# Third block of a two-network kernel on one Trainium2 core: five projection slabs as seven block products, probabilities scaled on ScalarE, another order at the feed-forward start and at the end

## The reference

```python
h = rms_norm_2(x, mix_norm_g[l]) * (1 + scale_m) + shift_m
proj = h @ w_in[l] + b_in[l]                       # 1024 -> 2816 columns
q_a, k_a, v_a, q_h, f_h, i_h, g_h = jnp.split(proj, IN_OFFSETS, axis=-1)
attn = sliding_window_gqa_with_sinks(q_a, k_a, v_a, sinks)   # p = e / (e.sum + exp(sink - m))
rec = hgrn2_chunkwise(q_h, f_h, i_h, lower_bounds)
rec = rms_norm_2(rec, hgrn_out_g) * jax.nn.silu(g_h)
x = x + gate_m * (concatenate([rms_norm_2(attn, attn_out_g), rec]) @ w_out[l])
h = rms_norm_2(x, ffn_norm_g[l]) * (1 + scale_f) + shift_f
u, v = jnp.split(h @ w_up[l], 2, axis=-1)          # 2 x 2816 columns
u = causal_depthwise_conv(u, conv_w[l], conv_b[l])
x = x + gate_f * ((jax.nn.silu(u) * v) @ w_down[l])
return rms_norm_2(x, final_norm_g)
```

## Time and profile before

| | |
|---|---|
| median of 3 runs (lowest to highest) | 1099.87 us (1098.5 to 1101.79) |
| profiled execution, its own time | 1098.37 us |
| its span | 1096.5 us |
| TensorE busy in the span | 1073.6 us, 98% |
| VectorE busy | 788.8 us, 72% |
| ScalarE busy | 332.0 us, 30% |

### The profile page before, as it was taken

The page is one execution under the profiler, slowest core; times in us unless marked ns, Lnnn a source line. Parts: engine busy times, 40 slices in busy tenths (PEclk is TensorE's granted clock), DMA queues, the critical chain, the costliest instruction groups (busy, mean ns, idle before and its releaser), DMA issues.

```text
span 1096.5 us, 18062 instructions
## 1 busy us (share of the span) xinstructions
PE 1073.6 (98%) x7396; PEld 972.1 (89%) x7396; DVE 788.8 (72%) x1359; ACT 332.0 (30%) x783; POOL 24.5 (2%) x83
## 2 busy tenths in 40 slices
PE   7999999999999999999999999999999999999997
PEld 4788888999999977888899999998889889999997
DVE  2477768888898848544779889887474288887755
ACT  3243324111111245663511111117343342222101
POOL 1000240000000000000000000000000000000000
PEclk9999999999999999999999999999999999999999
DMA  9899936898878662381868878774432165953411
GB/s 347 275 385 343 316 106 249 297 319 282 319 276 300 191 77 77 98 258 57 299 214 323 309 280 304 263 251 151 154 116 77 46 204 171 290 184 106 151 62 39
DMA packets 163011, 234.79 MB, mean 214 GB/s; under 512 B 8770, under 2 KB 137842, under 8 KB 162930
## 3 DMA queue, kind: packets, MB, share of 16 engines
q1 hardware_dynamic: 162572, 233.54, 63.2%
q10 hardware_dynamic: 357, 0.12, 0.0%
HBM read 232.19 MB, written 1.44 MB: 213 GB/s over the span
## 4 chain that ended last, share of the span: by engine, by line
PE 88%; DVE 8%; ACT 2%; issue 1%; ACTq 0%; DMA 0%; DVEq 0%
PE PS L850 34%; PE PS L780 13%; PE PS L896 13%; PE PS L808 7%; PE PS L971 6%; PE PS L1096 3%; PE PS L772 1%; PE PS L1358 1%; DVE hT L1978 1%; PE PS L793 1%; PE PS L701 1%; PE PS L1441 1%; DVE scratch L2400 1%; PE PS L1300 1%; PE PS L1049 1%
## 5 line engine op out<-in xcount | busy, mean ns | idle before, releaser
L780 PE MATMUL PS<-hT,slots 128*128 128x256 f32 x752 | 165.3, 380 | 0.8 <-ACT hT L1535 0.8
L780 PEld LDWEIGHTS PS<-hT,slots 128*128 128x128 f32 x752 | 142.1, 190 | 21.7 <-issue 2.9
L896 PE MATMUL PS<-act,slots 128*128 128x256 f32 x704 | 159.8, 380 | 0.4 <-DVE act L2123 0.4
L1902 DVE SCALAR_TENSOR_TENSOR ada_acc<-ada_slots,cond,ada_acc 128x1024 f32<-128x1024 f32 x119 | 152.4, 1280 | 4.8 <-DMA ada_slots<-in_ada_w 0.5
L896 PEld LDWEIGHTS PS<-act,slots 128*128 128x128 f32 x704 | 130.5, 190 | 18.9 <-issue 1.6
L1573 ACT ACTIVATE PS<-PS 128x128 f32<-128x128 f32 x180 | 53.5, 297 | 299.7 <-PE PS L850 299.7
L850 PE MATMUL PS<-oT,slots 128*128 128x128 f32 x960 | 126.9, 275 | 2.0 <-ACT PS L1573 2.0
L850 PE MATMUL PS<-hT,slots 128*128 128x128 f32 x960 | 127.0, 275 | 0.0
L850 PEld LDWEIGHTS PS<-hT,slots 128*128 128x128 f32 x960 | 119.6, 192 | 2.4
L850 PEld LDWEIGHTS PS<-oT,slots 128*128 128x128 f32 x960 | 116.8, 192 | 2.3 <-issue 2.3
L850 PE MATMUL PS<-oT,scratch 128*128 128x128 f32 x960 | 117.1, 275 | 0.0
(11 more groups left out here) (347 smaller groups left out, 1337.0 us busy)
## 6 DMA issues: line engine op xcount, KB each, us to landing
ada_slots<-in_ada_w SPq DMA_DIRECT2D x144, 512.0 KB, 8.6
slots<-in_ffn_w_up SPq DMA_DIRECT2D x44, 1024.0 KB, 11.9
slots<-in_ffn_w_down SPq DMA_DIRECT2D x22, 1024.0 KB, 5.0
slots<-in_w_up SPq DMA_DIRECT2D x22, 1024.0 KB, 5.2
slots<-in_sb_w_in SPq DMA_DIRECT2D x11, 1024.0 KB, 13.2
slots<-in_w_in SPq DMA_DIRECT2D x11, 1024.0 KB, 5.3
slots<-in_dsa_w_in SPq DMA_DIRECT2D x10, 1024.0 KB, 5.4
ada_slots<-in_w_down SPq DMA_DIRECT2D x2, 2816.0 KB, 12.4
```

The costliest lines, as they stand in the source:

```text
L780: last = mm(PS[:, bank, half * T:half * T + T], slot[s][:, k, m * P:(m + 1) * P], x[:, k, :], start=k == 0, stop=k == KC - 1)
L896: last = mm(PS[:, c // 2, (c % 2) * T:(c % 2) * T + T], w[:, j_odd * D + c * P:j_odd * D + (c + 1) * P], act[:, j_odd, :], start=start and ...
L1902: ins = dve.scalar_tensor_tensor(dst, ada_slot[k][:, :], c, dst, ALU.mult, ALU.add)
```

## The change

Five slabs of the third mixer no longer run as 16 matmuls of 256 columns but as 28 matmuls of 128 columns (`seven`), after the same scheme of block sums as the feed-forward. VectorE makes the sums of the activations once (`block_x_sums`) and of each slab's weights (`block_w_sums`), and puts the seven products together (`block_collect`). The probabilities are scaled by ScalarE (`window_scale`), the gate's SiLU reads VectorE's collected rows (`block_gate`). In the third feed-forward VectorE starts the sums of the first weight set before the last output slab, makes `norm` and `input_sums` before the two raw chunks, TensorE no longer waits for unit 3, and ScalarE takes the first two SiLUs after the first seeds. The output slabs 1 to 4 lie in slots 3, 4, 2, 5 where they lay in 2, 3, 4, 5. At the end one transpose moves into the last chain, `token_rows(0, 0)` moves ahead of the last `take`, and ScalarE's queue issues one of the four output transfers.

```diff
-OUT_SLOTS = ((3, 4, 5, 2), (3, 4, 5, 2), (2, 3, 4, 5))
+OUT_SLOTS = ((3, 4, 5, 2), (3, 4, 5, 2), (3, 4, 2, 5))
...
+                arrived(s)
+                fill(u)
+                product(0, w[:, 0:HALF, 0:P], b11, frees=frees)
+                product(1, w[:, HALF:KC, 0:P], b21)
+                pe.wait_ge(block_x_ready, 1)
+                pe.wait_ge(block_w_ready, bk("block_w_ready").next())
+                product(2, block_w[buf][1], block_x[1])
+                product(3, block_w[buf][0], block_x[0]).then_inc(block_half, 1)
+                product(4, w[:, 0:HALF, P:2 * P], block_x[2])
+                product(5, block_w[buf][2], b22)
+                product(6, w[:, HALF:KC, P:2 * P], block_x[3]).then_inc(unit_full[u], 1)
...
-            pair(3, 0, None)
-            tokens(4, 1, 3)
+            seven(3, 0, 0)
+            seven(4, 1, 1, frees=3, by_token=True)
             window_turn(4)
-            tokens(5, 0, None)
+            seven(5, 0, 2, by_token=True)
             window_mix(0, 1, 5)
             window_scores(1, None)
-            pair(0, 0, None)
-            pair(1, 1, 0)
+            seven(0, 0, 0)
+            seven(1, 1, 1, frees=0)
...
-                    if n == 0 and not j_odd:
+                    if l < 2 and n == 0 and not j_odd:
                         was_read(3)
...
+                    if p == 0:
+                        for raw_odd in (0, 1) if l == 2 else (1,):
+                            chunk(raw_odd)
+                            skip(2 + raw_odd)
...
+            def window_scale():
+                for m in range(2):
+                    act_e.wait_ge(inverse_ready, bk("inverse_ready").next())
+                    for e in range(2):
+                        for tt, (lo, hi_) in enumerate(((0, P), (P, 384))):
+                            x = esp[:, 2 * m + e, lo:hi_]
+                            last = act_e.activation(x, x, ACT.Copy, scale=psum_p[:, m, tt, e:e + 1])
+                    last.then_inc(p_ready, 1)
...
-            gate(hg, GH0, 0, ACT.Silu, 0)
-            gate(hg, GH0, 1, ACT.Silu, 1)
+            window_scale()
             window_probs()
+            block_gate(hg, GH0, 0, 0, 0)
+            block_gate(hg, GH0, 1, 1, 1)
...
+                act_e.wait_ge(block_taken, i + 1)
...
+            act_e.wait_ge(o_scaled, 1)
+            act_e.dma_start(out[0, P:2 * P, 0:512], oT_flat[:, 1024:1536]).then_inc(out_stored, 16)
...
+                if l == 2:
+                    weight_sums(2, 0, (1,))
+                    norm(1)
+                    input_sums()
+                    for odd in range(2):
+                        normalise(odd)
+                        chunk(odd, odd, raw[:, odd, 0, :], raw[:, odd, 1, :])
+                    weight_sums(2, 1, (0,))
+                    for odd in range(2):
+                        product(odd, normalised=True, j=odd)
+                    last_chunks()
+                    return
...
+                link(dve.tensor_tensor(s1, a21, a22, ALU.add))
+                dve.tensor_tensor(a21, a11, a21, ALU.subtract)
+                link(dve.tensor_tensor(s2, s1, a11, ALU.subtract))
+                dve.tensor_tensor(s4, a12, s2, ALU.subtract).then_inc(block_w_ready, 1)
...
+                dve.wait_ge(block_half, bk("block_half").next())
+                link(dve.tensor_copy(rows[:, 5 * P:6 * P], flat[:, 0:P]))
+                link(dve.tensor_tensor(rows[:, 0:8 * P].rearrange("p (a b) -> p a b", a=2)[:, :, 0:P], two(flat[:, P:3 * P]),
+                                       spread(rows[:, 5 * P:6 * P]), ALU.add))
                 full(u)
+                link(dve.tensor_tensor(two(rows[:, 6 * P:8 * P]), two(flat[:, 3 * P:5 * P]), spread(u2), ALU.add))
+                dve.tensor_tensor(rows[:, P:3 * P], flat[:, 5 * P:7 * P], rows[:, 6 * P:8 * P], ALU.add)
+                dve.tensor_tensor(rows[:, 3 * P:4 * P], flat[:, 3 * P:4 * P], rows[:, 7 * P:8 * P], ALU.add).then_inc(unit_read[u], 1)
...
-            values(0, 1)
+            values(0, 1, 1)
             decayed_halves(4)
-            values(1, 0)
+            block_w_sums(GH0, 0)
+            values(1, 0, 2)
             window_out(0, 1)
             window_max(1)
-            skip(0)
-            skip(1)
+            block_w_sums(GH0 + SLAB, 1)
             decayed_halves(5)
             decayed_near(6)
             window_norm()
+            for i in range(2):
+                block_collect(i, i)
+                dve.nop().then_inc(block_taken, 1)
...
-            out_projection(2, units=OUT_UNITS[2])
+            out_projection(2, units=OUT_UNITS[2], before_last=lambda: weight_sums(2, 0, (0,)))
```

More of the change, by code:

```diff
@@ L346, in build @@
         down_w_landed = {}
+        block_landed = {}
         def rows(ap):
@@ L968, in chain @@
                     for i in range(PAIRS):
-                        if i == PAIRS - 1 and late is not None:
+                        if i == late_at and late is not None:
                             late()
@@ L1006, in down_blocks @@
                     pe.wait_ge(s_sums_ready, 4 * b + 4)
[L1007 to L1010, removed]
+                    chain(b, 6, s_sum[2], acts[:, :, 1, P:T], late=turn_corner if b == 3 else None, late_at=8)
                 pe.wait_ge(x_turned, 12)
@@ L1350, in pair, with seven, product @@
                 project(2 * u + 1, s, 1, hT).then_inc(unit_full[u], 1)
-            def tokens(s, u, frees):
+            def seven(s, u, buf, frees=None, by_token=False):
+                w, flat = slot[s], PS[:, 2 * u:2 * u + 2, :].rearrange("p b n -> p (b n)")
+                b11, b21, b22 = hT[:, 0:HALF, 0:P], hT[:, HALF:KC, 0:P], hT[:, HALF:KC, P:T]
+                def product(r, a, b, frees=None):
+                    for k in range(HALF):
+                        lhs, rhs = (b[:, k, :], a[:, k, :]) if by_token else (a[:, k, :], b[:, k, :])
+                        last = mm(flat[:, r * P:(r + 1) * P], lhs, rhs, start=k == 0, stop=k == HALF - 1, skip_group_check=True)
+                        if k == 0 and frees is not None:
+                            last.then_inc(slot_used[frees], 1)
+                    return last
                 arrived(s)
                 fill(u)
[L1356 to L1362, removed]
+                product(0, w[:, 0:HALF, 0:P], b11, frees=frees)
[7 more added lines that the diff above has]
+                product(6, w[:, HALF:KC, P:2 * P], block_x[3]).then_inc(unit_full[u], 1)
             def window_keys(frees):
@@ L2003, in ffn, with token_rows @@
+            def token_rows(tt, half):
+                lo = half * 512
+                dve.scalar_tensor_tensor(oT_flat[:, tt * D + lo:tt * D + lo + 512], PS[:, 4 + 2 * tt + half, :], rtok[:, tt:tt + 1],
+                                         final_g[:, lo:lo + 512], ALU.mult, ALU.mult).then_inc(o_ready, 1)
             def ffn(l):
                 both = l < 2
[L2006 to L2022, removed]
@@ L2054, in normalise @@
                     full(2 + odd)
-                    if not odd:
+                    if not odd and both:
                         dve.wait_ge(rstd_ready, bk("rstd_ready").next())
@@ new lines, in block_w_sums @@
+            def block_w_sums(slab, buf):
+                s, landed = block_landed[slab]
+                dve.wait_ge(slot_loaded[s], landed)
+                w, (s1, s2, s4) = slot[s], block_w[buf]
+                a11, a12, a21, a22 = (w[:, k * HALF:(k + 1) * HALF, m * P:(m + 1) * P] for m in range(2) for k in range(2))
+                link(dve.tensor_tensor(s1, a21, a22, ALU.add))
+                dve.tensor_tensor(a21, a11, a21, ALU.subtract)
+                link(dve.tensor_tensor(s2, s1, a11, ALU.subtract))
+                dve.tensor_tensor(s4, a12, s2, ALU.subtract).then_inc(block_w_ready, 1)
@@ L2562, in window_out, with values @@
+            def values(i, u, buf):
+                rows = block_collect(u, buf)
+                bias = vi_bias[:, P + i * SLAB:P + (i + 1) * SLAB].rearrange("p (m c) -> p m c", m=2)
+                dve.tensor_tensor(hi_t[:, :, i * SLAB:(i + 1) * SLAB].rearrange("p t (m c) -> p m t c", m=2),
+                                  rows[:, 0:4 * P].rearrange("p (m t c) -> p m t c", m=2, t=2),
+                                  bias.unsqueeze(2).to_broadcast([P, 2, 2, P]), ALU.add)
             def window_out(i, u):
```

139 lines of the change are left out of this document (98 added, 41 removed).

## The result

The changed kernel took 1093.02 us (median of 4 runs, 1092.73 to 1093.89), the kernel before 1099.69 beside it (4 runs, 1098.5 to 1101.79): a ratio of 0.9939, 95% interval 0.9921 to 0.9956. The profiled execution took 1092.73 where that of before took 1098.37: 5.6 less, in a span of 1091.0 for 1096.5. One execution in the whole document, of its last kernel, was slow (1589.76 us at a mean granted clock of 0.657), and no comparison uses it.

What follows compares the result with a forecast made beforehand. The prediction took TensorE, busy 98% of the span, as the bound. Gains of 1.05 (mixer), 0.8 (feed-forward's start) and 0.8 (end) sum to 2.7 us: 1097.2 us against the median of 1099.87, 8-in-10 range 1094.3 to 1100.3.

Steps and rivals of the forecast that it cites:

- what bounds the kernel now: Whole kernel: TensorE, busy 98% of the span; idle entries read only at the third feed-forward's first product and the end.
- the sum of 2.7 us: Total predicted gain: 1.05 in the third mixer, 0.8 at the third feed-forward's start, 0.8 at the kernel's end.
- The slabs: Third mixer: 28 narrow matmuls take 6.25 us for 6.91, saving 0.66 a slab, 3.3 for five if TensorE never waits.
- VectorE's side: Third mixer: block sums cost 2.66 us and a collection 1.96, making unit 0 free at 815.8.
- the wait of 0.4: Third mixer, before the first gate slab: TensorE waits 0.4 us for VectorE to free unit 0, to 815.9.
- ScalarE's side: Third mixer: scaling, table load, gates and `cross` make TensorE wait 1.3 us before level 2; the mixer gains 1.05 of 3.3.
- Rival 3: Level 2 and the feed-forward's second slice: a table switch costs twice its load, another 1.28 us each; gain 0.1, chance 0.05.
- The feed-forward's start: Third feed-forward: the 1.43 us wait goes, new waits of 0.45 and 0.15 arise; gain 0.8, bounds 0 to 1.43.
- The end: End of the kernel: ScalarE's second root follows its own last sum, at about 1091.3 instead of 1092.13; gain 0.8 us.
- The two queues: End of the kernel: the last two 256 KB transfers leave from two queues at once, worth up to 0.3 us or nothing.
- the first: Rival: small instructions cheaper, collections at 1.5, VectorE never late; mixer gains 2.1, total 4.6, 1095.3 us; chance 0.33.
- The second: Rival: VectorE bounds the mixer at 3.65 us a collection; kernel 2.4 slower, 1102.3 us; chance 0.07.

Runs made afterwards that it cites:

- its last kernel: The changed kernel with levels copied ahead of the gates and the weight sums behind the sum of squares: 1090.46 us, ratio 0.9923 to the kernel before.

## Why the prediction was wrong

**The step that failed** is the first one, what bounds the kernel now. It said that TensorE has idle entries at two places, and costed ScalarE's new order only in the third feed-forward; in the first two it stood at nothing, without a reason. But the page of the kernel before has 2.0 us idle behind ScalarE's L1573 in one of its groups of seven-block products (L850), and those lie in the first two feed-forwards. The section on the reference says that the first two blocks are not touched, and that is wrong: the edit `if l < 2 and p:` changes both of their feed-forwards. Taking it back costs 2.3 to 2.7 us, alone on the kernel before it gives 2.7. Without it the sum of 2.7 us was nearly right (the traces give 3.0 for the same three terms); with the 2.56 it would have been 5.3.

**The slabs**: 6.25 each, as priced. **VectorE's side**: the collection takes 1.89 with the step to the next (810.77 to 812.66) for my 1.96, the sums 2.66 as priced. All small prices together were 0.6 us too high by unit 0's release (812.66 + 2.56 = 815.2 on the time axis of the kernel before, for 815.8), so the wait of 0.4 there did not arise (no idle entry at 812.95); the second turn lost 0.3, not 0.5. From the changed kernel's VectorE timeline:

```profile
810.77 0.28 DVE L2671 COPY oT<-PS 128x128 f32<-128x128 f32 x1
811.09 0.42 DVE L2672 TENSOR_TENSOR oT<-PS,oT 128x256 f32<-128x256 f32 x1
811.54 0.42 DVE L2675 TENSOR_TENSOR oT<-PS,oT 128x256 f32<-128x256 f32 x1
812.00 0.42 DVE L2676 TENSOR_TENSOR oT<-PS,oT 128x256 f32<-128x256 f32 x1
812.35 0.28 DVE L2677 TENSOR_TENSOR oT<-PS,oT 128x128 f32<-128x128 f32 x1
812.66 0.69 DVE L2684 TENSOR_TENSOR ada_acc<-oT,vi_bias 128x512 f32<-128x512 f32 x1
```

**ScalarE's side**: right in place and nearly in size. The wait before level 2 is 1.51 for 1.3. On the same axis level 2 starts at 834.6 for 834.8, so ScalarE was 0.2 early, and TensorE was ready at 833.1 for 833.5, so 0.4 early. ScalarE's timeline:

```profile
828.12 1.28 ACT L1841 ACT_TABLE_LOAD   x1
829.41 0.91 ACT L1841 ACTIVATE ada_acc<-scratch,pcol 128x256 f32<-128x256 f32 x2
830.35 0.91 ACT L1841 ACTIVATE ada_acc<-ffn_work,pcol 128x256 f32<-128x256 f32 x2
831.29 0.60 ACT L1882 ACTIVATE fm<-PS 128x512 f32<-128x512 f32 x1
```

The four gates take 1.88 and not 1.6: the second pair starts 0.94 after the first, and `cross` 0.94 after that, for the 0.80 that two unhindered instructions were priced at. By the code each of the two waits until the pair ahead of it has ended. The table's load ends at 829.40 and the gate starts at 829.41, so a switch cost the load alone; at the second slice of the feed-forward a load from 894.34 ends at 895.62 and the SiLU starts at 895.63. Rival 3 is out. By the drain of about 1.38 us that the Trainium skill (ScalarE: Activation LUTs, "What ACT_TABLE_LOAD costs") adds to each switch the gate would have started near 830.8, an estimate from the page's figure; the trace disagrees. The mixer gave 1.28 for 1.05.

**The feed-forward's start**: 0.80 for 0.8, with the terms right in kind and the agreement in part luck. The new wait of 0.45 is there, as 4.84 for 4.50 at the raw chunk and 0.17 at L779, but it cost 0.68 (5.01 for 4.33 from the raw chunk to L779), since slot 4's load left 0.4 later than I had taken it and the last addition was 1.2 late, not 0.9; from there to the first slice 1.49 was gained for the 1.43, and the second slice took 0.13 more, for the 0.15, made good by a first slice 0.14 shorter. **The end**: 0.9 for 0.8. The two queues, for which no row had a price, gave nothing: from ScalarE's last scaling to the end of the span it is 3.9 us in both kernels (1092.65 before, 1087.09 after). **Rivals**: the first came nearest in size (1095.3), and for the wrong reason. Of what it supposed, one wait of two did not arise, but a collection took 1.89 and not 1.5, and the mixer gave 1.28 and not 2.1. The second was not met, but with the scaling left on VectorE its mechanism shows. **What stays open**: the traces account for 5.5 us (2.56, 1.28, 0.80, 0.9) and the first medians differ by 6.7. The kernel before has single runs up to 3.3 us above its lowest and the changed one only 1.2; in the measurements that followed the kernel before was at 1098.4 to 1098.6, which gives 5.4 to 5.9. So some 1 us of the first difference is most likely the high median of the kernel before, to which the prediction was tied too. Why its runs spread wider was not tried.

## What to carry to other kernels

Read every wait of the engine that is the bound, over the whole program, before costing a diff, and lay each changed condition against that list: a reordering described for one stage may run in all of them. Block products save TensorE time only as far as the engines that make their sums have room; here 3.3 us saved became 1.28, and it came back (to some 2.7) when ScalarE copied first what TensorE waits for and loaded its table afterwards. An instruction moved to where its engine is idle is not free if it waits there for something that lands late, as the weight sums ahead of the last output slab did.

## What the runs showed of the hardware

A float32 matmul with 128 moving columns starts every 223 ns (6.25 us for 28) and one with 256 every 432 ns (6.91 for 16), so that halving the columns costs 3% here, at a mean granted clock of 0.997 (changed kernel) and 0.999 (before). It held for a slab made by features (788.86 to 795.11) and for one made by tokens (795.11 to 801.37) alike.

A table load took 1.28 us on ScalarE, and the next instruction began 0.01 later where it had nothing else to wait for (829.41 and 895.63 in the changed kernel, 842.50 before). A wait on TensorE cost a little more than its idle entry says: 1.22 for 1.05, and 1.14 for 0.98.
